# A two-layer diffusion trunk on one core: opening sequence, weight ring and the order of DVE at the norm boundaries changed together

## The chip, the cores and the metric

The kernel runs on one core of a Trainium2 chip. TensorE (PE) multiplies and writes PSUM; VectorE (DVE), ScalarE (ACT) and GpSimd (POOL) do the elementwise work; SyncE (SP) issues nearly all DMAs. The metric is the device time of one execution in microseconds. The kernel before takes 1502.31 us in the median of 3 runs (1501.9 to 1505.26).

## The reference, cut to what matters

384 tokens (128 of context, 256 latent) of width 1024 pass through two layers of three sub-layers each: feed-forward (FFN), mixer, FFN. The mixer of layer 0 is attention beside a convolution, that of layer 1 a Fourier mix beside a gated unit. Everything is float32.

```python
def modulate(x, g, shift, scale):
    return rms_norm(x, g) * (1 + scale) + shift
def swiglu(h, w_in, w_out):
    gate, up = jnp.split(h @ w_in, 2, axis=-1)
    return (jax.nn.silu(gate) * up) @ w_out
def macaron_layer(x, mod, norm_g, ffn_in, ffn_out, mixer):
    m = mod[:, :, None, :]
    x = x + 0.5 * m[:, 2] * swiglu(modulate(x, norm_g[0], m[:, 0], m[:, 1]), ffn_in[0], ffn_out[0])
    mixed, own_kv = mixer(modulate(x, norm_g[1], m[:, 3], m[:, 4]))
    x = x + m[:, 5] * mixed
    x = x + 0.5 * m[:, 8] * swiglu(modulate(x, norm_g[2], m[:, 6], m[:, 7]), ffn_in[1], ffn_out[1])
```

`mod` is `silu(cond) @ w_mod + b_mod`, nine vectors of 1024 for each layer and for each of two conditionings (`c_ctx` for the context, `c` for the latent tokens); FFN_DIM is 2816.

## The kernel before, in words

Activations lie transposed: features on the 128 partitions in KT = 8 tiles, tokens along the free axis. The weights come in 153 units of 128 x 2048 floats (1 MB). To keep float32 precision with the fast float32 form of TensorE, each unit is split: ACT rounds it (`w_hi`, L528), DVE subtracts (`w_lo`, L790). Every product is then three matmuls (function `three`, L1185 to L1187) of 384 columns, so one unit, 16 tiles of 128 x 128, is 48 matmuls. An FFN has 33 units (22 of its first matrix, 11 of its second), mixer 0 has 11, mixer 1 has 10.

Three rings of three buffers hold raw, high and low weights. SP loads unit u when DVE has split unit u-3 (`lo_done`); ACT splits it when it has landed and PE has used unit u-3.

The modulation matrix comes in two ways. The first 18 column tiles come as 9 "pairs" of 1 MB and go through PE (`mod_sums`, L1231, with `mod_columns`, L1241). The other 126 tiles (512 KB each) are multiplied and summed on DVE (`mod_tile`, L812, two instructions for a tile), spread over the FFNs by the tables TILES_BEFORE, TILE_LOOPS and TILES_OUT.

A norm boundary (five of them, numbered 1 to 5; norm 0 is the opening) runs so. The last unit of the sub-layer finishes its eight output tiles one by one (`y_done`); DVE adds each to x (`residual`, L852), ACT squares it (L538), POOL adds six of the squares (L453), PE sums over partitions (L1247), DVE and ACT make 1/rms (L861, L540, L864), DVE writes three diagonal matrices (L865), PE spreads them (L1254), and then DVE (L876), ACT (L546) and DVE (L883) make the operands `a_hi` and `a_lo` tile by tile, on which PE starts the next sub-layer. DVE computes the next shift and scale (`modulation_in`, L835 to L838) behind the residuals, and behind those it splits the second unit of the next sub-layer (`norm_stats(n, unit)`).

The opening brings x in by rows and transposes it on PE (L1350), brings the small vectors in by 13 DMAs from ACT's queue and transposes them (L1360, L1362), computes all 9 pairs, then norm 0, then unit 0. The end transposes x back (L1573), copies it (L773) and stores 3 x 512 KB (L436). The order on each engine is the order in which the code is written; nothing is scheduled by a program.

Of the kernel before, what the change touches and what calls it, by code (L numbers as in the profile page):

```python
# [20 lines left out]
FP32 = mybir.dt.float32  # L21
F32R = mybir.dt.float32r
# [4 lines left out]
P = 128  # L27
# [26 lines left out]
RING = 3  # L54
MRING = 3
UNIT = 2048
# [14 lines left out]
GROUPS_FIRST = 3  # L71
LOOPS = (FT - 1) // RING
FIRST_TILES = MRING * GROUPS_FIRST * PAIR_TILES
MOD_TILES = 2 * MODT - FIRST_TILES
TILES_BEFORE = {0: 3, 2: 0, 3: 0, 5: 2}
TILE_LOOPS = {0: LOOPS, 2: LOOPS, 3: LOOPS, 5: 2}
TILES_OUT = {0: [3, 3] + [2] * 8, 2: [2] + [1] * 9, 3: [3] + [2] * 8 + [0], 5: [0] * 10}
TILE0, _t = {}, 0
for _s in (0, 2, 3, 5):
    TILE0[_s] = _t  # L80
    _t += TILES_BEFORE[_s] + MRING * TILE_LOOPS[_s] + sum(TILES_OUT[_s])
assert _t == MOD_TILES and MRING == RING
# [3 lines left out]
COND_AT = 2 * (MRING - 1)  # L86
# [83 lines left out]
def build(nc, x_prompt, x_sample, cache_k, cache_v, c, c_ctx, b_mod, norm_g,  # L170
          q_norm_g, k_norm_g, conv_w, conv_b, conv_norm_g, conv_norm_b,
          sgu_norm_g, sgu_norm_b, sgu_w, sgu_b, k_ident, k_rope, k_fourier, w_units, w_pairs, w_rows,
          y_prompt, y_sample, new_cache_k, new_cache_v):
    ctx = ExitStack()
    with ctx:
# [117 lines left out]
        out_in, out_t, out_c, out_done = sem("out_in"), sem("out_t"), sem("out_c"), sem("out_done")  # L293
# [38 lines left out]
        def mod_rows(b):  # L332
            return m_raw[:, b, 0:D_MODEL]

        def cond_row(cnd):
            return m_raw[:, cnd, D_MODEL:UNIT]

        def row_products():
            return m_raw[:, 2, D_MODEL:UNIT]
# [3 lines left out]
        def _(sp):  # L343
            def load_unit(u, i=0):

                sp.wait_ge(lo_done, u + 1 + RING * i)
                sp.dma_start(w_raw[:, slot(u), :].unsqueeze(1),
                             w_units[bass.ds(u + i * RING, 1)].rearrange("u p n -> p u n")).then_inc(raw_in[slot(u)], 16)

            def load_pair(group, b, i=0):  # L350

                sp.wait_ge(mod_used, MRING * group + b + 1 + MRING * i)
                sp.dma_start(m_raw[:, b, :].unsqueeze(1),
                             w_pairs[bass.ds(MRING * group + b + i * MRING, 1)].rearrange("u p n -> p u n")
                             ).then_inc(mod_in[b], 16)

            def load_tile(n, i=0):

                if n >= MRING:
                    sp.wait_ge(tile_used, n - MRING + 1 + MRING * i)  # L360
                sp.dma_start(mod_rows(n % MRING).unsqueeze(1),
                             w_rows[bass.ds(n + MRING * i, 1)].rearrange("t p n -> p t n")).then_inc(tile_in[n % MRING], 16)

            def load_ffn(s):
                u0, n = UNIT0[s], TILE0[s]

                if s == 0:
                    for pair in range(MRING, MRING * GROUPS_FIRST):
                        if pair == MRING * GROUPS_FIRST - 2:
                            load_unit(u0)  # L370
                        load_pair(pair // MRING, pair % MRING)
                else:
                    load_unit(u0)
                load_unit(u0 + 1)
                load_unit(u0 + 2)
                if s == 0:
                    sp.wait_ge(mod_used, MRING * (GROUPS_FIRST + 1))
                    for cnd, src in enumerate((c_ctx.unsqueeze(0), c)):
                        sp.dma_start(cond_row(cnd), src.to_broadcast([P, D_MODEL])).then_inc(rows_in, 16)
# [4 lines left out]
                for rounds, with_tiles in ((TILE_LOOPS[s], True), (LOOPS - TILE_LOOPS[s], False)):  # L384
                    if rounds:
                        with sp.Fori(0, rounds) as i:
                            for b in range(RING):
                                load_unit(u0 + 3 + RING * done + b, i)
                                if with_tiles:
                                    load_tile(n + b, i)  # L390
                        done += rounds
                n += MRING * TILE_LOOPS[s]
                for j, tiles in enumerate(TILES_OUT[s]):
                    if j < FFN_OUT_UNITS - 2:
                        load_unit(u0 + FT + 2 + j)
# [3 lines left out]

            sp.dma_start(ident[:], k_ident).then_inc(const_in, 16)  # L400
            sp.dma_start(cond_rows[0:KT, :], c_ctx.rearrange("(r n) -> r n", n=P)).then_inc(cond_in, 16)
            sp.dma_start(cond_rows[KT:2 * KT, :], c[0].rearrange("(r n) -> r n", n=P)).then_inc(cond_in, 16)
            for b in range(MRING):
                load_pair(0, b)
            sp.dma_start(x_nat[:, 0, :], x_prompt[0]).then_inc(x_in, 16)
            sp.dma_start(x_nat[:, 1:TT, :], x_sample[0].rearrange("(a p) n -> p a n", p=P)).then_inc(x_in, 16)
# [26 lines left out]
            for tt in range(TT):  # L433
                sp.wait_ge(out_c, tt + 1)
                dst = y_prompt[0] if tt == 0 else y_sample[0, (tt - 1) * P:tt * P, :]
                sp.dma_start(dst, x_nat[:, tt, :]).then_inc(out_done, 16)  # L436
            sp.wait_ge(out_done, 16 * TT)
# [4 lines left out]
        def _(pool):  # L442
# [12 lines left out]
            add_squares(0)  # L455
# [32 lines left out]
            pool.wait_ge(acc_done, (ADDED - 1) * 5)  # L488
# [1133 lines left out]
```

## Time and profile before

| what | value |
|---|---|
| median of 3 runs | 1502.31 us |
| profiled execution | 1499.5 us, of it span 1497.7 us |
| PE busy | 1407.8 us (94%) |
| DVE busy | 970.0 us (65%) |
| ACT / POOL busy | 557.7 us / 122.5 us |
| chain that ended last | PE 83%, DVE 10%, DMA 2%, ACT 2% |
| granted clock, mean | 0.964 |

A stretch in which PE is busy for its whole length can't be shortened by other engines; where it is not, the row of the timeline names in square brackets the idle time before an instruction and what ended it.

### The profile page before, as it was taken

The page shows a single profiled execution, that of the slowest core. Times are in us where ns is not written, and L with a number is a line of the kernel's source. Part 1 is how long each engine was busy: PE and PEld are TensorE (multiplying, and loading weights), DVE is VectorE, ACT ScalarE, POOL GpSimd, SP SyncE. Part 2 cuts the span into 40 slices and gives each one's busy share as a digit, 9 for nine tenths or more (in the row PEclk, how much of TensorE's full clock was granted, in tenths as well). Part 3 has the DMA queues.
Part 4 walks back from the last instruction along what each step waited for, and adds up shares of the span by engine and source line. Part 5 has one row for each costly group of instructions (what it writes and reads, how often), then busy time and mean ns, then how long its engine had stood idle before and what let it go on. Part 6 is the DMA issues. An engine that isn't in the chain of part 4 may idle for free.

```text
span 1497.7 us, 21193 instructions
## 1 busy us (share of the span) xinstructions
PE 1407.8 (94%) x8134; PEld 1375.4 (92%) x8134; DVE 970.0 (65%) x1394; ACT 557.7 (37%) x731; POOL 122.5 (8%) x110
## 2 busy tenths in 40 slices
PE   5799999989866899999998999999989989999998
PEld 3799999989845799999998999999989989999998
DVE  2777678968998566666757666679763477444332
ACT  2433332237666443333224333332345343333221
POOL 1000000014555100000001000000021010000000
PEclk9899999989878999999998999999989999999999
DMA  8765655752200235555652555547523325433421
GB/s 325 261 231 176 203 177 200 285 182 96 86 32 29 102 133 201 188 191 174 234 181 85 197 193 185 193 149 295 219 99 134 126 85 186 137 122 130 141 84 42
DMA packets 45114, 242.96 MB, mean 162 GB/s; under 512 B 4997, under 2 KB 6889, under 8 KB 24328
## 3 DMA queue, kind: packets, MB, share of 16 engines
q1 hardware_dynamic: 44464, 241.99, 46.7%
q8 instruction: 32, 0.52, 0.1%
q10 hardware_dynamic: 600, 0.30, 0.1%
q14 instruction: 18, 0.15, 0.0%
HBM read 240.57 MB, written 1.70 MB: 162 GB/s over the span
## 4 chain that ended last, share of the span: by engine, by line
PE 83%; DVE 10%; DMA 2%; ACT 2%; issue 1%; POOL 1%; ACTq 0%; SPq 0%; DVEq 0%; POOLq 0%
PE ps L1185 27%; PE ps L1186 27%; PE ps L1187 27%; DVE conv L974 4%; DVE w_lo L790 1%; DMA conv_rows<-in_conv_w 1%; DVE n_full L876 1%; PE ps L1254 1%; DVE m_raw L812 1%; DVE smax L1039 1%; ACT w_hi L528 1%; DVE a_lo L883 0%; POOL n_acc L453 0%; DMA m_raw<-in_w_pairs 0%; PE ps L1554 0%
## 5 line engine op out<-in xcount | busy, mean ns | idle before, releaser
L1185 PE MATMUL ps<-a_hi,w_hi 128*128 128x384 f32 x1744 | 591.7, 339 | 19.1 <-DVE a_lo L883 14.0
L1186 PE MATMUL ps<-a_lo,w_hi 128*128 128x384 f32 x1744 | 588.5, 337 | 0.0
L1187 PE MATMUL ps<-a_hi,w_lo 128*128 128x384 f32 x1744 | 588.1, 337 | 0.0
L790 DVE TENSOR_TENSOR w_lo<-w_raw,w_hi 128x2048 fp32r<-128x2048 f32 x153 | 352.9, 2306 | 162.3 <-ACT w_hi L528 162.0
L528 ACT ACTIVATE w_hi<-w_raw 128x2048 fp32r<-128x2048 f32 x153 | 292.1, 1909 | 264.7 <-PE ps L1187 200.2
L1185 PEld LDWEIGHTS ps<-a_hi,w_hi 128*128 128x128 f32 x1744 | 332.1, 190 | 23.4 <-issue 10.0
L1186 PEld LDWEIGHTS ps<-a_lo,w_hi 128*128 128x128 f32 x1744 | 332.1, 190 | 0.1
L1187 PEld LDWEIGHTS ps<-a_hi,w_lo 128*128 128x128 f32 x1744 | 331.7, 190 | 0.0
L812 DVE SCALAR_TENSOR_TENSOR m_raw<-m_raw 128x1024 f32<-128x1024 f32 x252 | 296.0, 1220 | 1.0 <-ACT m_raw L589 1.0
L1187 PE MATMUL ps<-h_hi,w_lo 128*128 (+1 forms) x704 | 236.6, 336 | 0.0
L1186 PE MATMUL ps<-h_lo,w_hi 128*128 (+1 forms) x704 | 236.6, 336 | 0.0
L1185 PE MATMUL ps<-h_hi,w_hi 128*128 (+1 forms) x704 | 236.6, 336 | 0.0
L557 ACT ACTIVATE glu<-ps 128x384 f32<-128x384 f32 x88 | 43.4, 493 | 376.6 <-PE ps L1187 376.6
L895 DVE TENSOR_TENSOR glu<-glu,ps 128x384 f32<-128x384 f32 x88 | 48.7, 554 | 167.2 <-ACT glu L557 167.2
L1187 PEld LDWEIGHTS ps<-h_hi,w_lo 128*128 128x128 f32 x704 | 132.4, 188 | 0.0
L1185 PEld LDWEIGHTS ps<-h_hi,w_hi 128*128 128x128 f32 x704 | 132.4, 188 | 0.0
L1186 PEld LDWEIGHTS ps<-h_lo,w_hi 128*128 128x128 f32 x704 | 132.4, 188 | 0.0
L898 DVE TENSOR_TENSOR h_lo<-glu,h_hi 128x384 f32 (+1 forms) x88 | 49.2, 559 | 71.6 <-ACT h_hi L559 71.6
L453 POOL TENSOR_TENSOR n_acc<-n_sq 128x384 f32<-128x384 f32 x6 | 6.1, 1014 | 973.4 <-ACT n_sq L538 879.5
L559 ACT ACTIVATE h_hi<-glu 128x384 f32 (+1 forms) x88 | 46.2, 525 | 86.4 <-DVE glu L895 86.4
L473 POOL TENSOR_TENSOR conv<-conv,taps_buf 128x399 f32<-128x399 f32 x60 | 72.9, 1215 | 51.5 <-ACT taps_buf L618 45.6
L974 DVE SCALAR_TENSOR_TENSOR conv<-padded,conv_wt,conv 128x399 f32<-128x399 f32 x60 | 61.1, 1018 | 1.6
(179 smaller groups left out, 666.2 us busy)
## 6 DMA issues: line engine op xcount, KB each, us to landing
w_raw<-in_w_units SPq DMA_DIRECT2D x153, 1024.0 KB, 5.0
m_raw<-in_w_rows SPq DMA_DIRECT2D x126, 512.0 KB, 3.6
m_raw<-in_w_pairs SPq DMA_DIRECT2D x9, 1024.0 KB, 7.7
out<-x_nat SPq DMA_DIRECT2D x3, 512.0 KB, 3.1
x_nat<-in_x_sample SPq DMA_DIRECT2D x1, 1024.0 KB, 12.5
fourier<-in_k_fourier SPq DMA_DIRECT2D x1, 768.0 KB, 4.4
x_nat<-in_x_prompt SPq DMA_DIRECT2D x1, 512.0 KB, 10.7
m_raw<-in_c_ctx SPq DMA_DIRECT2D x1, 512.0 KB, 5.7
```

The costliest lines, as they stand in the source:

```text
L473: nc.gpsimd.tensor_tensor(acc, acc, taps_buf[:, n % TAP_BUFS, :], ALU.add).then_inc(tap_added, 1)
L528: nc.scalar.activation(w_hi[:, slot(u), :], w_raw[:, slot(u), :], ACT.Copy).then_inc(hi_done, 1)
L557: nc.scalar.activation(glu[:, 0, :], ps[:, 2 * b, 0:TOK], ACT.Silu).then_inc(silu_done, 1)
L559: nc.scalar.activation(h_hi[:, bass.ds(t + RING * i, 1), :], glu[:], ACT.Copy).then_inc(h_hi_done, 1)
L790: nc.vector.tensor_tensor(w_lo[:, slot(u), :], w_raw[:, slot(u), :], w_hi[:, slot(u), :].bitcast(FP32), ALU.subtract).then_inc(lo_done, 1)
L812: nc.vector.scalar_tensor_tensor(out, mod_rows(n % MRING), 1.0, cond_row(cnd), ALU.mult, ALU.mult, accum_out=mod_cols[:, bass.ds(FIRST_TIL ...
L895: nc.vector.tensor_tensor(glu[:, 0, :], glu[:, 0, :], ps[:, 2 * b + 1, 0:TOK], ALU.mult).then_inc(prod_done, 1)
L898: nc.vector.tensor_tensor(h_lo[:, bass.ds(t + RING * i, 1), :], glu[:], h_hi[:, bass.ds(t + RING * i, 1), :].bitcast(FP32), ALU.subtract). ...
L974: ins = nc.vector.scalar_tensor_tensor(conv[:, j, :], padded[:, j, k:k + CONV_N], conv_wt[:, j, k:k + 1], conv[:, j, :], ALU.mult, ALU.add)
L1185: mm(out, whi, mhi, start=start, stop=False)
L1186: mm(out, whi, mlo, start=False, stop=False)
L1187: return mm(out, wlo, mhi, start=False, stop=stop)
```

## The change

It does several things in one edit.

1. **Ring.** One ring of four slots in place of three rings of three: `w_lo` lies over `w_raw`, so DVE subtracts in place. A unit is loaded when PE has finished unit u-4 (`unit_done`). The FFN loops turn by four units, and PSUM banks rotate over four steps.
2. **Opening.** Host code hands x, the conditionings and all vectors over already in columns, so the transposes and ACT's 13 DMAs go; the pairs are 8, each with one shift and one scale tile of the same feature tile k; PE works through them one by one between the matmuls of units 0 and 1, which now run together. The squares of norm 0 are all summed on PE.
3. **End.** SP stores x in eight pieces of 192 KB straight behind each residual; no transposes, no copies.
4. **Tiles.** 128 tiles on DVE, 1, 2, 1, 2 in the four steps of a loop; three tiles come in step 1 of FFN 0, not ahead of step 0.
5. **Boundary.** DVE's split of the second unit of the next sub-layer, the gate and `modulation_in` stand ahead of the residuals.

```diff
-RING = 3
+RING = 4
+TRING = 3
+STEP_TILES = [1, 2, 1, 2]
-TILES_BEFORE = {0: 3, 2: 0, 3: 0, 5: 2}
+TILES_BEFORE = {0: TRING, 2: 0, 3: 0, 5: 2}
+TILES_OUT = {0: [2] * 7 + [1, 0, 0], 2: [1, 1] + [0] * 8, 3: [2] * 5 + [0] * 5, 5: [0] * 10}
...
             def load_unit(u, i=0):
-                sp.wait_ge(lo_done, u + 1 + RING * i)
+                sp.wait_ge(unit_done, u + 1 + RING * i)
...
+                    load_pair(0)
+                    load_unit(u0)
+                    load_unit(u0 + 1)
+                    for k in range(1, KT):
+                        load_pair(k)
+                    load_unit(u0 + 2)
...
+            for d in range(KT):
+                sp.wait_ge(x_ready, KT * N_SUB + d + 1)
+                sp.dma_start(y_cols[:, d, :], x[:, d, :]).then_inc(out_done, 16)
...
             norm_stats(0)
             split(0)
-            norm(0)
+            norm(0, 0, 1)
             split(1)
+            norm(0, 1, KT)
+            split(2)
...
+                if s < 5:
+                    split(u0 + FFN_UNITS + 1)
                 modulation_gate(s)
+                if s < 5:
+                    modulation_in(s + 1)
                 for d in range(KT):
...
                     residual(s, d)
-                if s < 5:
-                    modulation_in(s + 1)
...
+            for k in range(KT):
+                if k + 2 < KT:
+                    mod_sums(k + 2)
+                pe.wait_ge(a_ready, k + 1)
+                for m in range(2):
...
+                    for h in range(2):
+                        ins = three(ps[:, 2 * m + h, 0:TOK], tile_of(w_hi, m, h * KT + k), tile_of(w_lo, m, h * KT + k),
+                                    a_hi[:, k, :], a_lo[:, k, :], k == 0, k == KT - 1)
...
+                if k + 2 < KT:
+                    mod_columns(k + 2)
```

DVE's order at the boundary from FFN 0 to mixer 0. Before, the last tiles, the gate, the residuals, shift and scale, then the split:

```order
L790 TENSOR_TENSOR w_lo<-w_raw,w_hi 128x2048
L812 SCALAR_TENSOR_TENSOR m_raw,mod_cols<-m_raw 128x1024 x4
L844 TENSOR_TENSOR m_gate<-mod_cols,vec_a 128x16
L847 TENSOR_SCALAR m_gate<-m_gate 128x16
L852 SCALAR_TENSOR_TENSOR x<-ps,m_gate,x 128x128
...
L835 TENSOR_TENSOR m_shift<-mod_cols,vec_a 128x16
L836 TENSOR_TENSOR m_scale<-mod_cols,vec_a 128x16
L838 SCALAR_TENSOR_TENSOR m_scale<-m_scale,vec_a 128x16
L790 TENSOR_TENSOR w_lo<-w_raw,w_hi 128x2048
L861 TENSOR_SCALAR stat<-ps 128x3
```

In the changed kernel the same place reads (L767 is the split, L789 a tile, L826 a residual, L833 the statistic):

```order
L789 SCALAR_TENSOR_TENSOR m_raw,mod_cols<-m_raw 128x1024 x2
L767 TENSOR_TENSOR w_lo<-w_raw,w_hi 128x2048 x3
L818 TENSOR_TENSOR m_gate<-mod_cols,vec_a 128x16
L821 TENSOR_SCALAR m_gate<-m_gate 128x16
L809 TENSOR_TENSOR m_shift<-mod_cols,vec_a 128x16
L810 TENSOR_TENSOR m_scale<-mod_cols,vec_a 128x16
L812 SCALAR_TENSOR_TENSOR m_scale<-m_scale,vec_a 128x16
L826 SCALAR_TENSOR_TENSOR x<-ps,m_gate,x 128x128
...
L833 TENSOR_SCALAR stat<-ps 128x3
```

The split and the three small instructions went ahead of the sixteen residuals, and no tile is left behind the last two units.

PE's order in the opening. Before:

```order
L1231 MATMUL ps<-m_raw,cond 32x256 x24
L1350 MATMUL ps<-ident,x_nat 128x128 x24
L1241 MATMUL ps<-mod_pick,mod_part 128x6 x2
L1231 MATMUL ps<-m_raw,cond 32x256 x8
L1247 MATMUL ps<-ones,n_sq 128x1 x6
L1247 MATMUL ps<-ones,n_acc 128x1 x3
L1360 MATMUL ps<-ident,rows 128x120
...
L1231 MATMUL ps<-m_raw,cond 32x256 x24
L1241 MATMUL ps<-mod_pick,mod_part 128x6 x2
L1185 MATMUL ps<-a_hi,w_hi 128x384
```

Now (L1224 is a pair's sums, L1234 its columns, L1240 the sum over partitions, L1177 the first matmul of a product):

```order
L1224 MATMUL ps<-m_raw,cond 32x256 x8
L1234 MATMUL ps<-mod_pick,mod_part 128x2 x2
L1240 MATMUL ps<-ones,n_sq 128x1 x24
L1247 MATMUL ps<-n_diag,ones 128x128 x3
L1224 MATMUL ps<-m_raw,cond 32x256 x8
L1234 MATMUL ps<-mod_pick,mod_part 128x2 x2
L1224 MATMUL ps<-m_raw,cond 32x256 x8
L1177 MATMUL ps<-a_hi,w_hi 128x384
...
L1234 MATMUL ps<-mod_pick,mod_part 128x2 x2
L1224 MATMUL ps<-p_raw,cond 32x256 x8
L1177 MATMUL ps<-a_hi,w_hi 128x384
```

The first product now stands behind three pairs, not nine, and five pairs lie between the products.

SP's order in the opening, changed kernel (L350 loads a unit, L354 a pair, L378 the conditioning rows, L360 a tile; the branch opens the loop of FFN 0):

```order
L406 DMA x<-in_x_cols 128x3072
L354 DMA m_raw<-in_w_pairs 128x2048
L350 DMA w_raw<-in_w_units 128x2048 x2
L354 DMA m_raw<-in_w_pairs 128x2048 x2
L354 DMA p_raw<-in_w_pairs 128x2048 x5
L350 DMA w_raw<-in_w_units 128x2048
...
L378 DMA m_raw<-in_c 128x1024
L360 DMA m_raw<-in_w_rows 128x1024 x3
L389 UNCONDITIONAL_BRANCH
```

Before, it read:

```order
L353 DMA m_raw<-in_w_pairs 128x2048 x3
L405 DMA x_nat<-in_x_prompt 128x1024
L406 DMA x_nat<-in_x_sample 128x2x1024
L353 DMA m_raw<-in_w_pairs 128x2048 x4
L347 DMA w_raw<-in_w_units 128x2048
L353 DMA m_raw<-in_w_pairs 128x2048 x2
L347 DMA w_raw<-in_w_units 128x2048 x2
```

x and the first two units moved to the front, and the tile of step 2 is queued ahead of the load of unit 4.

## Rows read from the trace of the kernel before

**Rows 1.** Windows: length, busy of PE, PEld, DVE, ACT, POOL; granted clock; DMA.

```profile
39.00:42.00 3.00, 2.40 (x19) 1.07 (x19) 0.42 (x1) 0.00 (x0) 0.00 (x0) 0.50 0.97 407
160.00:280.00 120.00, 120.00 (x695) 120.00 (x694) 92.71 (x123) 37.72 (x34) 0.00 (x0) 1.00 0.60 203
```

**Rows 2.** Timeline of PE, opening: start, us, engine, line, what, [idle before, releaser].

```profile
7.56 1.93 PE L1231 MATMUL ps<-m_raw,cond 128*32 128x256 f32 x16 [4.03 <-DMA m_raw<-in_w_pairs]
12.71 1.93 PE L1231 MATMUL ps<-m_raw,cond 128*32 128x256 f32 x16 [0.73 <-DMA m_raw<-in_w_pairs]
22.90 1.50 PE L1247 MATMUL ps<-ones,n_sq 128*128 128x1 f32 x12
27.57 1.35 PE L1254 MATMUL ps<-n_diag,ones 128*128 128x128 f32 x6
32.55 0.61 PE L1241 MATMUL ps<-mod_pick,mod_part 128*128 128x6 f32 x4 [0.56 <-DVE mod_part L797]
33.09 1.07 PE L1231 MATMUL ps<-m_raw,cond 128*32 128x256 f32 x16
41.53 1.02 PE L1241 MATMUL ps<-mod_pick,mod_part 128*128 128x6 f32 x4 [0.55 <-DVE mod_part L797]
67.53 0.45 PE L1185 MATMUL ps<-a_hi,w_hi 128*128 128x384 f32 x1 [1.60 <-DVE w_lo L790]
```

**Rows 3.** Timeline of DVE and ACT: one step of FFN 0.

```profile
93.41 0.55 DVE L895 TENSOR_TENSOR glu<-glu,ps 128x384 f32<-128x384 f32 x1 [1.61 <-ACT glu L557]
94.53 1.90 ACT L528 ACTIVATE w_hi<-w_raw 128x2048 fp32r<-128x2048 f32 x1
95.27 1.22 DVE L812 SCALAR_TENSOR_TENSOR m_raw<-m_raw 128x1024 f32<-128x1024 f32 x1
97.56 2.29 DVE L790 TENSOR_TENSOR w_lo<-w_raw,w_hi 128x2048 fp32r<-128x2048 f32 x1
```

**Rows 4.** Timeline, boundary 3 (FFN 2 to FFN 3); last product ends 801.75.

```profile
799.02 4.47 POOL L453 TENSOR_TENSOR n_acc<-n_acc,n_sq 128x384 f32<-128x384 f32 x4
803.83 0.81 PE L1247 MATMUL ps<-ones,n_acc 128*128 128x1 f32 x6
805.97 0.15 DVE L861 TENSOR_SCALAR stat<-ps 128x3 f32<-128x3 f32 x1
811.10 0.66 PE L1185 MATMUL ps<-a_hi,w_hi 128*128 128x384 f32 x1 [2.23 <-DVE a_lo L883]
```

**Rows 5.** Timeline, boundary 1 (FFN 0 to mixer 0); last product ends 325.73.

```profile
322.78 5.29 DVE L852 SCALAR_TENSOR_TENSOR x<-ps,m_gate,x 128x128 f32<-128x128 f32 x16
325.97 6.48 POOL L453 TENSOR_TENSOR n_acc<-n_acc,n_sq 128x384 f32<-128x384 f32 x4
332.50 1.44 PE L1247 MATMUL ps<-ones,n_acc 128*128 128x1 f32 x6 [1.96 <-POOL n_acc L453]
```

**Rows 6.** Timeline of DVE and PE, boundaries 2 (519) and 5 (1207).

```profile
517.48 0.81 PE L1247 MATMUL ps<-ones,n_acc 128*128 128x1 f32 x6
519.48 0.15 DVE L861 TENSOR_SCALAR stat<-ps 128x3 f32<-128x3 f32 x1
1206.52 0.81 PE L1247 MATMUL ps<-ones,n_acc 128*128 128x1 f32 x6
1207.84 0.15 DVE L861 TENSOR_SCALAR stat<-ps 128x3 f32<-128x3 f32 x1
```

**Rows 7.** Timeline, the end; last product ends 1489.07.

```profile
1489.11 0.74 DVE L852 SCALAR_TENSOR_TENSOR x<-ps,m_gate,x 128x128 f32<-128x128 f32 x2 [0.30 <-PE ps L1187]
1491.04 2.86 ACT L773 ACTIVATE x_nat<-ps 128x1024 f32<-128x1024 f32 x3 [24.91 <-PE ps L1573]
```

**Rows 8.** DMA issues, first 75 us and whole span: what, count, KB each, us to landing.

```profile
ident<-in_k_ident SPq DMA_DIRECT2D x1, 64.0 KB, 1.9
...
w_raw<-in_w_units SPq DMA_DIRECT2D x153, 1024.0 KB, 5.0
...
out<-x_nat SPq DMA_DIRECT2D x3, 512.0 KB, 3.1
```

More of the change, by code:

```diff
@@ L432, in _ @@
             load_ffn(5)
[L433 to L437, printed above, removed]
+            for d in range(KT):
+                sp.wait_ge(x_ready, KT * N_SUB + d + 1)
+                sp.dma_start(y_cols[:, d, :], x[:, d, :]).then_inc(out_done, 16)
+            sp.wait_ge(out_done, 16 * KT)
             sp.wait_ge(cache_out, 32)
@@ L540, in norm_stats, with norm @@
                 nc.scalar.activation(stat[:, 4:4 + TT], stat[:, 0:TT], ACT.Sqrt).then_inc(root_done, 1)
-            def norm(n):
-                for d in range(KT):
+            def norm(n, d0=0, d1=KT):
+                for d in range(d0, d1):
                     for cnd, lo, hi in SEGS:
@@ L770, in _ @@
             ffn(5)
-            for tt in range(TT):
-                act.wait_ge(out_t, tt + 1)
-                nc.scalar.activation(x_nat[:, tt, :].rearrange("p (a b) -> p a b", a=2), ps[:, 2 * tt:2 * tt + 2, :],
-                                     ACT.Copy).then_inc(out_c, 1)
         @block.vector
@@ L854, in residual, with norm_stats @@
                 ins.then_inc(x_ready, 1)
-            def norm_stats(n, unit=None):
-                if unit is not None:
-                    split(unit)
+            def norm_stats(n):
                 dve.wait_ge(stat_done, n + 1)
@@ L900, in step @@
                                             ALU.subtract).then_inc(h_ready, 1)
-                    if tile is not None:
+                    for tile in tiles:
                         mod_tile(tile, i)
+                step(0, 0, 0, [])
                 if s == 0:
                     dve.wait_ge(silu_rows, 2)
-                for _ in range(TILES_BEFORE[s]):
-                    mod_tile(n)
-                    n += 1
-                step(0, 0, 0, None)
+                step(1, 1, 0, range(n, n + TILES_BEFORE[s]))
+                n += TILES_BEFORE[s]
                 done = 0
@@ L914, in ffn @@
                             for b in range(RING):
-                                step(1 + RING * done + b, (1 + b) % RING, i, n + b if with_tiles else None)
+                                at = n + sum(STEP_TILES[:b])
+                                step(2 + RING * done + b, (2 + b) % RING, i, range(at, at + STEP_TILES[b] * with_tiles))
                         done += rounds
-                n += MRING * TILE_LOOPS[s]
+                n += sum(STEP_TILES) * TILE_LOOPS[s]
                 for j, tiles in enumerate(TILES_OUT[s]):
@@ L1303, in ffn @@
                 pe.wait_ge(h_ready, 1 + FT * (f + 1))
-                with pe.Fori(0, (FFN_OUT_UNITS - 2) // RING) as i:
+                rounds = (FFN_OUT_UNITS - 2) // RING
+                with pe.Fori(0, rounds) as i:
                     for b in range(RING):
                         out_unit(u0 + FT + 1 + b, 1 + b, i)
+                for t in range(1 + RING * rounds, FFN_OUT_UNITS - 1):
+                    out_unit(u0 + FT + t, t, 0)
                 u = u0 + FFN_UNITS - 1
```

378 lines of the change are left out of this document (173 added, 205 removed).

## The prediction

> **What bounds the kernel now.** I read the page first: PE is busy 94% of the span and holds 83% of the chain, so only stretches in which it waits can give time. The windows then show where it does not wait: from 160 to 280 us PE is busy for all of 120 us, 695 matmuls at 172.7 ns, so a unit of 48 takes 8.3 us [rows 1]. The timeline of PE shows the same for all four FFNs from the fourth unit on, so a deeper ring gains nothing inside an FFN. PE waits in the opening, at five norm boundaries, in the attention and at the end. The attention (DVE and ACT chains) keeps its instructions; I cost it at nothing, since a unit there is loaded earlier than it is split in any case, and DVE, which sets its pace, has the same list.
>
> **The end.** Before, the last residual ends at 1489.85, the last of three copies at 1493.90, and a store of 512 KB takes 3.1 us to land [rows 7, 8]: 1497.0, plus 0.7 to the end of the span. Now the last piece of 192 KB is issued at 1489.9. Its landing lies between the 1.9 us of 64 KB and the 3.1 us of 512 KB [rows 8]; I take 2.3, nearer to the small one. End at 1489.9 + 2.3 + 0.7 = 1492.9: **4.8 us saved** (4.0 to 5.2). The Trainium skill, DMA: Bandwidth & Descriptors, Anatomy of one DMA, gives about 2.0 us fixed plus bytes over 436 GB/s for a DMA from GpSimd's queue, an estimate of 2.45 us here; by it the end would save 4.65 us. No row has a piece of this size.
>
> **The boundaries.** At boundary 3 PE has the sum over partitions done at 803.83 + 0.81 = 804.64, but DVE reads it only at 805.97, because it is still in the split that stands in front [rows 4]. With split and modulation ahead of the residuals DVE reads at once, 0.05 us later: 1.28 saved. Boundary 4 has the same instructions in the same order between two FFN-like stages: 1.28 again. Boundary 2: 519.48 - 518.29 less 0.05 = 1.14. Boundary 5: 1207.84 - 1207.33 less 0.05 = 0.46 [rows 6]. Nothing else is behind DVE there, so what is late next is the unchanged chain of 1/rms, spread and first `a_lo`.
>
> Boundary 1 is different. DVE comes to its residuals only at 322.78, from its tiles, while y's first tile was there 7.3 us before the last product's end, at 318.4 [rows 5]. POOL's four adds then take 6.48 us where boundary 3 has 4.47, and PE's sum is done at 333.94, 8.21 us after its last product; at boundary 3 it is 2.89 us [rows 4, 5]. The new table leaves DVE no tile behind the last three units, so boundary 1 should look like boundary 3: 8.21 - 2.89 = **5.3 saved**. Why POOL is slow matters a little. Its adds lie beside DVE's split, which follows residuals that end at 328.07 [rows 5]; those of boundary 3 lie ahead of the split. The Trainium skill, SBUF — State Buffer, Who interferes with whom, says that a DVE `tensor_tensor` with both inputs in SBUF locks out GpSimd's reads for the whole instruction; the trace agrees, 2.0 us more on four adds. If the adds stayed slow for another reason, the accumulation started on time at 321.9 would end at 329.4 and the sum at 330.2 in place of 328.6, and 3.7 would be saved.
>
> Does the moved split delay the residuals? It needs unit u-4 done, that is two units, 16.6 us, before the boundary's last product ends. Load 5.0 [rows 8], ACT 1.90, DVE 2.29 [rows 3], five small instructions 1.0: ready 10.3 us later with issue time. At an FFN's end the first y comes 9.4 us after that point. DVE starts its residuals 0.9 late, but needs 0.74 for one against 1.04 between two y, and has caught up by the fourth. Behind a mixer the first four residuals wait and the last four do not. Sum of the boundaries: 5.3 + 1.14 + 1.28 + 1.28 + 0.46 = **9.5 us saved** (8 to 10).
>
> **The opening.** Before, PE starts unit 2 at 67.53 [rows 2] and runs on without a gap, so unit 4 starts at 67.53 + 2 x 8.32 = 84.2. Now, in order:
>
> DMA: the first pair landed at 7.56, the third 5.15 later, so 2.58 us for a MB [rows 2]. x (1.5 MB) is first: 8.9. Pair 0 11.4, unit 0 14.0, unit 1 16.6, pair 1 19.2, pair 7 34.7, unit 2 37.3.
>
> PE: pair 0's sums 11.4 to 13.4 (1.93, the slow row), DVE's copy 0.43, columns 1.02 [rows 2]: 15.0. Then the sums of eight tiles of squares. At 2.4 GHz two tiles took 1.50, so eight take 6.0 [rows 2]. At 1.2 GHz one took 1.44 [rows 5], so eight take 11.5; the granted clock of such a stretch is 0.50 in the window at 39 [rows 1]. I take 7.5, near the fast row, since at 22.90 as well PE had just come through other small matmuls. 22.5. Statistic and diagonals 1.2 (805.97 to the spread at boundary 3), spread 1.35 [rows 2]: 25.1. ACT splits unit 0 at 22.9 to 24.8, DVE to 27.1; tile 0 of norm 0 and pair 1's copy to 28.9; columns to 29.95, shift and scale to 30.3. DVE's split of unit 1 ends at 32.6 and the first product starts there.
>
> From there PE is the bound: 96 products' matmuls 16.6, five pairs 5 x 1.07, six columns 6 x 0.61 [rows 2], and 1.7 for the first 3 us at the low clock: 27.3. Units 0 and 1 end at 59.9. The pairs have all landed by 34.7, so the DMAs don't bind. Unit 2 is split by ACT only behind norm 0's last tile, and by DVE behind that: 1.5 us after PE is free, start 61.4.
>
> Then a new wait. Step 1 puts three tiles (3 x 2.29) on DVE. The first is used 10.8 us after unit 2's start, counted in the order of the code: ACT's table load and two SiLU of the conditioning rows end at +1.0, step 0 at +2.6, ACT's split of unit 3 at +4.5, DVE's at +6.8, step 1's product and low part at +8.5, the tile at +10.8 [rows 3]. SP holds the load of unit 4 behind a fourth tile, which waits for that buffer. The load takes 5.5, the splits 4.3 with hand-over: unit 4 starts 20.9 us after unit 2, where PE was free after 16.6. **A stall of 4.3 us.** Unit 4 starts at 82.3 against 84.2: **1.9 saved**. Afterwards DVE needs 15.2 us for two steps (two of 4.15 with one tile, and one tile more [rows 3]) out of 16.6, and works its backlog off; units 5 to 9 come 2 to 4 us ahead of PE's need.
>
> Bounds: without the stall and with fast sums 7.7 saved; with all sums slow (+4.0) and a round trip through DVE of 0.8 us in each of six rounds, 6.9 lost.
>
> **Sum.** 4.8 + 9.5 + 1.9 = 16.2 us. The profiled execution took 1499.5 with 1.8 outside its span; it would take 1483.3. The median of the runs is 2.8 above it, so the time is 1502.3 - 16.2 = 1486.1 us.
>
> **Rivals.**
> (a) The stall at unit 4 does not come, because the load lands sooner or DVE's step 1 is shorter. For it: DMA share is free by then. Against: the tile's wait stands in SP's order. 1502.3 - 20.5 = 1481.8.
> (b) The streamed opening is slow: sums at 1.2 GHz and each round waits for DVE (scale, `a_hi`, `a_lo` in turn). For it: the window at 39 us shows 0.50 for just such pair work [rows 1]. Then the opening loses 6.9 and the time is 1502.3 - 14.3 + 6.9 = 1494.9. The Trainium skill, TensorE: Matmul & The Clock Gate, Part 1, says that the slow clock is the default and activity releases it; by that rule too a thin opening stays slow.
> (c) Slower than before: the FFN loops are no longer free of gaps. A unit is now loaded only once PE has left its slot, and SP holds it behind tiles; DVE has 15.2 of 16.6 us filled in FFN 0, 2 and 3, where it had 2 x 4.15 = 8.3 plus split waits. If contention or register work adds more than 1.4 us to two steps, PE waits. At 1 us too much for each of 30 pairs of steps it costs 30: 1516. Against: DVE's rows are steady to 0.01 us and the unit needed has 8 us of slack in my count.
> (d) The boundary part doesn't do what it says, because the split waits for its load and pushes the residuals: boundaries gain only boundary 1's backlog, 3.7, so 1502.3 - 10.4 = 1491.9.
>
> **How the numbers follow.** Forecast 0.55, (a) 0.15, (b) 0.16, (c) 0.07, (d) 0.07. The forecast's own range is 1482 to 1490. The range of all is 1478 to 1496; it leaves out (c) and the tails of (a) and (b). A change of 0.2%, 3 us, is what a measurement of this kernel can tell from none. Faster: all but (c) and a tenth of (b), 0.91. Same 0.03. Slower 0.06.
>
> **What would show it.** Unit 2 starting near 61 and a PE idle of about 4 us ahead of unit 4, ended by DVE's split and that by a landing; no idle from there to 320. At each boundary, DVE's statistic within 0.1 us of PE's sum, and PE idle plus norm work of about 8.1 us between last and first product in place of 9.35 [rows 4], at boundary 1 too. Residuals of FFN ends 1.04 us apart from the fourth on. The span ending 3 us after the last residual. The forecast is wrong if gaps of PE appear inside FFN 2, 3 or 5, or if the first product starts after 37 us.

## The result, and the profile after

The changed kernel takes 1561.89 us (median of 4 runs, 1556.95 to 1569.81) against 1502.29 us for the kernel before, run beside it: ratio 1.0397, 95% interval 1.0352 to 1.0443. It is slower by 4%, where 1486.1 us, faster than before, was forecast.

I cut the profiled executions at the same places of the program: the start of TensorE's first product and the end of its last one in each sub-layer, and in FFN 0 also the start of unit 4. Times in us; the last column is the kernel of the first experiment, which changes SyncE's order alone.

| stage | before | after | units first |
|---|---|---|---|
| opening, to the start of unit 4 | 84.29 | 85.10 | 80.25 |
| FFN 0 from unit 4 | 241.44 | 283.91 | 241.57 |
| boundary 1 | 13.30 | 7.67 | 7.26 |
| mixer 0 | 176.37 | 177.70 | 180.85 |
| boundary 2 | 9.21 | 8.06 | 7.69 |
| FFN 2 | 277.14 | 289.79 | 276.53 |
| boundary 3 | 9.35 | 8.21 | 8.07 |
| FFN 3 | 277.26 | 305.70 | 277.54 |
| boundary 4 | 9.36 | 8.09 | 7.52 |
| mixer 1 | 106.72 | 106.48 | 106.12 |
| boundary 5 | 8.52 | 8.06 | 8.07 |
| FFN 5 | 276.10 | 276.18 | 277.58 |
| end | 8.64 | 3.05 | 3.06 |
| span | 1497.7 | 1568.0 | 1482.1 |

The boundaries gained 9.6, where 9.5 was forecast, and the end 5.6, where 4.8 was. Three of the four FFNs lost 42.5, 12.7 and 28.4: 83.6 us. They are the three that carry nearly all modulation tiles; FFN 5, with 8 tiles of the 128, lost nothing. Below, the in phase of an FFN is its first 22 units, the out phase its last 11.

The page of the changed kernel, its costliest groups (busy us, mean ns | idle before them, and what ended it). Before, ACT's split waited 264.7 us, 200.2 of them for PE; now it waits for the landing of the unit and for nothing else, while its busy time is as before (292.1 us then):

```profile
L767 DVE TENSOR_TENSOR w_lo<-w_raw,w_hi 128x2048 fp32r<-128x2048 f32 x153 | 352.9, 2309 | 343.9 <-ACT w_hi L512 343.6
L512 ACT ACTIVATE w_hi<-w_raw 128x2048 fp32r<-128x2048 f32 x153 | 292.8, 1914 | 421.3 <-DMA w_raw<-in_w_units 421.3
```

Windows of the changed kernel, columns as in [rows 1]. Where TensorE was busy for all of a window before, it is now busy 65.74 of 79 us at the end of FFN 0 and 67.31 of 75 in FFN 3; in FFN 2's out phase, which has no tiles by then, it is full. The window at 84, around the gap of 4.43 us ahead of unit 4, has the granted clock at 0.50, so this gap costs more than its own length.

```profile
84.00:89.00 5.00, 3.90 (x12) 3.90 (x13) 4.17 (x6) 2.15 (x2) 0.00 (x0) 0.50 0.27 111
290.00:369.00 79.00, 65.74 (x336) 64.18 (x336) 50.51 (x72) 20.20 (x17) 4.07 (x4) 0.91 0.45 173
780.00:850.00 70.00, 70.00 (x406) 70.00 (x405) 22.87 (x24) 19.00 (x15) 2.10 (x3) 1.00 0.37 130
1090.00:1165.00 75.00, 67.31 (x368) 66.37 (x367) 39.47 (x52) 21.49 (x17) 3.04 (x3) 0.95 0.47 174
```

The timeline of PE after, at unit 2, at unit 4 and at four of the 15 gaps of over 0.8 us that lie further inside the FFNs:

```profile
63.74 0.44 PE L1177 MATMUL ps<-a_hi,w_hi 128*128 128x384 f32 x1 [1.23 <-DVE w_lo L767]
85.10 0.69 PE L1177 MATMUL ps<-a_hi,w_hi 128*128 128x384 f32 x1 [4.43 <-DVE w_lo L767]
...
761.44 0.69 PE L1177 MATMUL ps<-h_hi,w_hi 128*128 128x384 f32 x1 [5.69 <-DVE glu L873]
1056.18 0.69 PE L1177 MATMUL ps<-h_hi,w_hi 128*128 128x384 f32 x1 [5.82 <-DVE glu L873]
1085.93 0.68 PE L1177 MATMUL ps<-h_hi,w_hi 128*128 x1 [5.80 <-DVE w_lo L767]
1111.58 0.68 PE L1177 MATMUL ps<-h_hi,w_hi 128*128 x1 [4.12 <-DVE w_lo L767]
```

Each is ended by DVE, by a split or by the last `glu` of an in phase. But DVE was idle before its split, as one unit of FFN 3's out phase shows (timeline of DVE, ACT and SyncE's queue; L789 is a tile's product, L360 issues a tile, L350 a unit):

```profile
1096.43 2.29 DVE L767 TENSOR_TENSOR w_lo<-w_raw,w_hi 128x2048 fp32r<-128x2048 f32 x1 [6.07 <-ACT w_hi L512]
1098.64 1.22 DVE L789 SCALAR_TENSOR_TENSOR m_raw<-m_raw 128x1024 f32<-128x1024 f32 x1
1099.79 1.22 DVE L789 SCALAR_TENSOR_TENSOR m_raw<-m_raw 128x1024 f32<-128x1024 f32 x1
1101.04 0.33 SPq L360 DMA_DIRECT2D m_raw<-in_w_rows  x1
1101.41 0.48 SPq L350 DMA_DIRECT2D w_raw<-in_w_units  x1
1107.18 1.91 ACT L512 ACTIVATE w_hi<-w_raw 128x2048 fp32r<-128x2048 f32 x1 [10.78 <-DMA w_raw<-in_w_units]
1109.13 2.29 DVE L767 TENSOR_TENSOR w_lo<-w_raw,w_hi 128x2048 fp32r<-128x2048 f32 x1 [5.82 <-ACT w_hi L512]
```

Read it as a circle, a chain of waits that closes on itself. Split 2.21, one tile 2.40 to its release, the next tile's issue 0.37, unit issued and landed 5.77, ACT 1.95, and DVE's next split: 12.70 us, against 8.3 that PE needs. The unit stands in SyncE's queue behind a tile, the tile waits for the tile three back, and DVE comes to that one only behind the split of the unit before. No engine is full: DVE idles 5.8 us in each turn. In the in phase, two steps with three tiles turn the same circle in 17.5 us (splits at 1018.40, 1035.97 and 1053.36, the one between each two left out), where PE needs 16.6:

```profile
1018.40 2.29 DVE L767 TENSOR_TENSOR w_lo<-w_raw,w_hi 128x2048 fp32r<-128x2048 f32 x1 [2.35 <-ACT w_hi L512]
...
1035.97 2.29 DVE L767 TENSOR_TENSOR w_lo<-w_raw,w_hi 128x2048 fp32r<-128x2048 f32 x1 [2.50 <-ACT w_hi L512]
...
1053.36 2.29 DVE L767 TENSOR_TENSOR w_lo<-w_raw,w_hi 128x2048 fp32r<-128x2048 f32 x1 [2.32 <-ACT w_hi L512]
```

That eats DVE's lead over PE at 0.9 us per pair of steps, until PE waits for the last `glu` of the in phase: the gaps of 5.69 and 5.82. In the kernel before, the unit needed next was issued one step earlier against the tiles, ahead of them.

### The profile page after: what moved, and what is told of

It reads as the page before. It is cut to its first block, busy times and chain, and to the rows that moved or that the text cites. A ratio compares the mean times of both kernels' runs of the same rounds, so it can differ in the third digit from the quotient of the medians.

```text
span 1568.0 us, 21066 instructions
## 1 busy us (share of the span) xinstructions
PE 1438.7 (92%) x8113; PEld 1398.6 (89%) x8113; DVE 971.6 (62%) x1410; ACT 556.1 (35%) x725; POOL 113.8 (7%) x105
## 4 chain that ended last, share of the span: by engine, by line
PE 46%; DVE 16%; DMA 16%; issue 11%; ACT 8%; SPq 1%; DVEq 1%; POOL 0%; ACTq 0%; POOLq 0%
DMA w_raw<-in_w_units 16%; PE ps L1177 14%; PE ps L1179 14%; PE ps L1178 14%; DVE m_raw L789 6%; ACT w_hi L512 5%; DVE conv L964 4%; DVE w_lo L767 2%; PE ps L1240 1%; DVE glu L873 1%; ACT h_hi L544 1%; SPq L360 1%; DMA m_raw<-in_w_pairs 1%; PE ps L1224 1%; PE ps L1247 1%
## 5 line engine op out<-in xcount | busy, mean ns | idle before, releaser
L1177 PE MATMUL ps<-a_hi,w_hi 128*128 128x384 f32 x1744 | 595.9, 342 | 22.8 <-DVE a_lo L851 11.1
L767 DVE TENSOR_TENSOR w_lo<-w_raw,w_hi 128x2048 fp32r<-128x2048 f32 x153 | 352.9, 2309 | 343.9 <-ACT w_hi L512 343.6
L1177 PEld LDWEIGHTS ps<-a_hi,w_hi 128*128 128x128 f32 x1744 | 333.5, 191 | 35.3 <-DVE w_lo L767 16.1
L789 DVE SCALAR_TENSOR_TENSOR m_raw<-m_raw 128x1024 f32<-128x1024 f32 x256 | 299.2, 1220 | 0.0
L1177 PE MATMUL ps<-h_hi,w_hi 128*128 (+1 forms) x704 | 246.3, 350 | 49.2 <-DVE w_lo L767 32.2
L1178 PE MATMUL ps<-h_lo,w_hi 128*128 (+1 forms) x704 | 243.6, 346 | 0.0
L1179 PE MATMUL ps<-h_hi,w_lo 128*128 (+1 forms) x704 | 243.5, 346 | 0.0
L1177 PEld LDWEIGHTS ps<-h_hi,w_hi 128*128 128x128 f32 x704 | 138.2, 196 | 54.4 <-issue 36.6
L1178 PEld LDWEIGHTS ps<-h_lo,w_hi 128*128 128x128 f32 x704 | 138.3, 196 | 0.0
L1179 PEld LDWEIGHTS ps<-h_hi,w_lo 128*128 128x128 f32 x704 | 137.7, 196 | 0.0
```

The lines of the kernel that those rows point to most:

```text
L767: nc.vector.tensor_tensor(w_lo[:, slot(u), :], w_raw[:, slot(u), :], w_hi[:, slot(u), :].bitcast(FP32), ALU.subtract).then_inc(lo_done, 1)
L789: nc.vector.scalar_tensor_tensor(out, mod_rows(n % TRING), 1.0, cond_row(cnd), ALU.mult, ALU.mult, accum_out=mod_cols[:, bass.ds(FIRST_TIL ...
L1177: mm(out, whi, mhi, start=start, stop=False)
L1178: mm(out, whi, mlo, start=False, stop=False)
L1179: return mm(out, wlo, mhi, start=False, stop=stop)
```

## The experiments

The theory is the circle through SyncE's queue. Rival 1: DVE has too much work. Rival 2: in the ring of four shared slots a load starts only when PE has left the slot, and that is too late. Rival 3 came up later: a unit issued one step later is itself too late, whatever the tiles wait for.

**Units first.**

```diff
+                load_unit(u0 + 3)
                 for _ in range(TILES_BEFORE[s]):
                     load_tile(n)
...
-                                load_unit(u0 + 3 + RING * done + b, i)
+                                load_unit(u0 + 4 + RING * done + b, i)
...
-                    load_unit(u0 + FT + 1 + j)
+                    if j < FFN_OUT_UNITS - 2:
+                        load_unit(u0 + FT + 2 + j)
```

> The changed kernel with SyncE's order alone changed: every unit of an FFN is issued one step earlier against the modulation tiles, so the load of unit t+2 stands ahead of the tiles of step t and no longer behind them. Nothing else moves, the tiles and the work of DVE are the same. Theory (a closed chain through SyncE's queue: a tile's load waits for the tile three back, the unit's load stands behind it, and DVE's use of that tile stands behind the split of the unit): the idle times of PE inside FFN 0, 2 and 3 (42.4, 12.7 and 28.4 us longer than where no tile is) go, and of the 4.4 us ahead of unit 4 about 1 us stays; 1561.9 - 83.5 - 3.3 = 1475 us. Rival 1 (DVE is too full: 15.2 us of work in 16.6, and glu and h_lo come late): DVE's work is the same, so the gaps stay, 1555 to 1562 us. Rival 2 (a load can start only when PE has left the slot, since raw and low part share four slots): that wait is the same, so the gaps stay but for the one ahead of unit 4, about 1558 us.

Measured: 1483.89 us (1480.64 to 1485.47), ratio to before 0.9872 (0.9852 to 0.9891). No gap of PE inside any FFN is left but 1.23 and 0.54 us ahead of units 2 and 4, with DVE's list and the slots unchanged, so rivals 1 and 2 fall as causes of the gaps. Its windows:

```profile
160.00:280.00 120.00, 120.00 (x694) 120.00 (x693) 102.49 (x138) 37.11 (x33) 0.00 (x0) 1.00 0.67 234
290.00:321.00 31.00, 31.00 (x181) 31.00 (x180) 14.80 (x26) 10.32 (x11) 3.38 (x4) 1.00 0.38 132
1010.00:1079.00 69.00, 69.00 (x400) 69.00 (x399) 38.39 (x51) 19.97 (x16) 3.42 (x4) 1.00 0.45 165
```

The span fell from 1568.0 to 1482.1, by 85.9 where I expected 86.8. The time expected (1475) was still 9 us too low, because I took stage losses from the profiled execution, 1569.8 us, off the median of the runs, 1561.9.

**Short tiles.** Only this is edited (the modulation is computed from 64 of its 1024 terms):

```diff
-                        out, mod_rows(n % TRING), 1.0, cond_row(cnd), ALU.mult, ALU.mult,
+                        out[:, 0:64], mod_rows(n % TRING)[:, 0:64], 1.0, cond_row(cnd)[:, 0:64], ALU.mult, ALU.mult,
```

> The changed kernel with each modulation tile's two products on DVE cut from 1024 columns to 64 (the modulation is then computed from 64 of its 1024 terms); loads, waits and order are as in the changed kernel. A tile should take DVE some 0.3 us in place of 2.3. Theory (the chain through SyncE's queue): it still runs load about 6, ACT 1.95, DVE's split 2.2, a short tile 0.3, issue 0.5 = 10.7 to 11 us per unit in the out phase, against PE's 8.3: gaps of PE stay in the out phases of FFN 0 and 3, but shorter, some 2.4 us for each of seven and five units less a lead of up to 8 us, and the in phase has none: 1490 to 1500 us. Rival 1 (DVE too full): DVE has 9 us of 16.6, so no gap is left at all, 1475 to 1480 us. Rival 2 (slots): as before, 1555 us or more.

Measured: 1508.02 us (1505.65 to 1514.22), ratio 1.0042 (1.0028 to 1.0057), 8 us over the theory's range and 28 over rival 1's. Both ranges stood on the base that the first experiment showed to be 9 us too low. The circle turns as worked out, 10.73 and 10.66 us in FFN 0's out phase, with DVE idle for 7.8 of them:

```profile
288.17 2.29 DVE L767 TENSOR_TENSOR w_lo<-w_raw,w_hi 128x2048 fp32r<-128x2048 f32 x1 [7.81 <-ACT w_hi L512]
298.90 2.29 DVE L767 TENSOR_TENSOR w_lo<-w_raw,w_hi 128x2048 fp32r<-128x2048 f32 x1 [7.81 <-ACT w_hi L512]
309.56 2.29 DVE L767 TENSOR_TENSOR w_lo<-w_raw,w_hi 128x2048 fp32r<-128x2048 f32 x1 [7.74 <-ACT w_hi L512]
```

So emptying DVE about halves each turn's excess over 8.3 (from 4.4 to 2.4) and doesn't end it: most of the circle is the load and the two splits. The gaps left inside FFN 0 and 3 are 0.5 to 3.6 us each, 14.6 in sum, and these FFNs take 25 us more than with the units first.

**Late units in the kernel before.** The inverse: in the kernel before, each unit is issued one step later against the tiles.

```diff
                 load_unit(u0 + 1)
-                load_unit(u0 + 2)
...
-                                load_unit(u0 + 3 + RING * done + b, i)
+                                load_unit(u0 + 2 + RING * done + b, i)
...
-                    if j < FFN_OUT_UNITS - 2:
-                        load_unit(u0 + FT + 2 + j)
+                    load_unit(u0 + FT + 1 + j)
```

> The kernel before with SyncE's order alone changed, the other way round: every unit of an FFN from the third on is issued one step later against the tiles, so it stands behind the tiles of the step before, as in the changed kernel. Its three slots, separate raw buffers and one tile per step stay. Theory (the chain through SyncE's queue): the in phase has one tile per step and three tile buffers, so its tile waits three steps back and the loop stays free of gaps; the out phases of FFN 0 (3, 3 and eight times 2 tiles) and FFN 3 (3 and eight times 2) come to 13 to 15 us per unit against 8.3: 25 to 50 us longer in each, 1540 to 1590 us; FFN 2 and 5 within 3 us of before. Rival 1 (DVE too full through 1, 2, 1, 2 tiles) and rival 2 (shared slots): neither is in this kernel, so 1502 to 1506 us.

Measured: 1599.91 us (1598.45 to 1600.92), ratio 1.0648 (1.0628 to 1.0669), 10 us past the upper end. FFN 0 (from its first product) and FFN 3 lost 44.1 and 37.6, inside the 25 to 50 expected of each; the boundaries behind them lost another 11.9 and 3.9, which I had not priced. DVE's splits in FFN 3's out phase stand 12.56 and 12.68 apart, as in the changed kernel, though this one has three rings of three slots:

```profile
1106.33 2.29 DVE L788 TENSOR_TENSOR w_lo<-w_raw,w_hi 128x2048 fp32r<-128x2048 f32 x1 [5.82 <-ACT w_hi L526]
1118.89 2.29 DVE L788 TENSOR_TENSOR w_lo<-w_raw,w_hi 128x2048 fp32r<-128x2048 f32 x1 [5.68 <-ACT w_hi L526]
1131.57 2.29 DVE L788 TENSOR_TENSOR w_lo<-w_raw,w_hi 128x2048 fp32r<-128x2048 f32 x1 [5.81 <-ACT w_hi L526]
```

FFN 2, with one tile per unit (two at one of them), takes 277.1 us (580.94 to 858.04), as before. The late order and several tiles per unit suffice for the loss; the ring of four is not needed for it.

**Six tile buffers.** The changed kernel, SyncE's order as it is:

```diff
-        m_raw = sb("m_raw", [P, MRING, UNIT])
+        m_raw = sb("m_raw", [P, MRING + 2, UNIT])
-TRING = 3
+TRING = 6
-TILES_BEFORE = {0: TRING, 2: 0, 3: 0, 5: 2}
+TILES_BEFORE = {0: 3, 2: 0, 3: 0, 5: 2}
```

with the waits on `tile_used` shifted by six to match. A tile then waits for the tile six back.

> The changed kernel with six buffers for modulation tiles in place of three, and SyncE's order left as it is: each unit's load still stands behind the tiles of the step before. A tile's load now waits until DVE has used the tile six back, three or four steps earlier. Theory (a closed chain, tile used, next tile issued, unit behind it issued, landed, split, tile used): with six buffers the chain closes over three steps instead of one, so the gaps of PE inside FFN 0, 2 and 3 go and the stall ahead of unit 4 shrinks to about 1 us, as with the units issued first: 1480 to 1488 us. Rival 3 (issuing a unit a step later is itself too late, whatever the tiles wait for): gaps stay, 1545 us or more. Rival 2 (slot free only when PE has left it): gaps stay, 1555 us or more.

Measured: 1480.95 us (1480.65 to 1484.04), ratio 0.9862 (0.9847 to 0.9878). The gaps are gone with the units still issued late, so rival 3 falls, rival 2 once more, and the wait of the tile is what closes the circle:

```profile
290.00:320.00 30.00, 30.00 (x175) 30.00 (x174) 13.02 (x23) 10.39 (x11) 3.37 (x4) 1.00 0.37 128
1010.00:1076.00 66.00, 66.00 (x383) 66.00 (x382) 35.30 (x49) 19.54 (x16) 3.69 (x4) 1.00 0.38 128
```

**Units first, residuals first.** DVE's order at all boundaries as before, on top of the first experiment:

```diff
-                if s < 5:
-                    split(u0 + FFN_UNITS + 1)
                 modulation_gate(s)
-                if s < 5:
-                    modulation_in(s + 1)
...
                     residual(s, d)
+                if s < 5:
+                    modulation_in(s + 1)
+                    split(u0 + FFN_UNITS + 1)
```

> The kernel with the units first, and in it DVE's order at all five norm boundaries as in the kernel before: residuals, then the next norm's shift and scale, then the split of the unit. Against the kernel with the units first it prices that part of the change alone. By the prediction's terms: statistic read 1.28 later at boundaries 3 and 4, 1.14 at 2, 0.46 at 5, and 1.28 at boundary 1, whose backlog of tiles is gone in both: 5.4 us slower. Rival (the split ahead of the residuals delays them and gives nothing, or gives more because POOL's adds no longer lie beside the split): within 1 us of it, or 8 to 10 us slower.

Measured: 1485.76 us (1483.82 to 1486.39), ratio 0.9883 (0.9866 to 0.9900): 1.9 us above the units first, which the intervals don't tell from nothing. The traces price the order directly. With the split ahead, DVE reads the statistic 0.04 us after PE's sum at all five boundaries; here it reads it 0.15 after at boundary 1 and 0.51 at the other four. That makes 2.0 us, not 5.4, and agrees with the 1.9 between the medians. (The five boundaries take 8.44, 8.51, 8.53, 8.53 and 8.34, 3.7 more in sum than in the execution of the units first. But with the split ahead the same sum lies anywhere from 38.6 to 40.1 us in the profiled executions of five kernels, so single executions can't price it closer than 2.3 to 3.7.)

So part of what I had priced as DVE's order goes without it. Boundary 3 of the kernel before, and then of this one (ACT's last split ahead of the boundary, its table load, DVE's second small instruction; then PE's sum and the statistic):

```profile
793.53 1.92 ACT L528 ACTIVATE w_hi<-w_raw 128x2048 fp32r<-128x2048 f32 x1 [6.46 <-PE ps L1187]
795.46 1.28 ACT L532 ACT_TABLE_LOAD   x1
802.53 0.99 DVE L836 TENSOR_TENSOR m_scale<-mod_cols,vec_b 128x16 f32<-128x16 f32 x1
```

```profile
783.92 1.92 ACT L514 ACTIVATE w_hi<-w_raw 128x2048 fp32r<-128x2048 f32 x1 [6.35 <-DMA w_raw<-in_w_units]
785.85 1.28 ACT L518 ACT_TABLE_LOAD   x1
796.36 0.16 DVE L812 TENSOR_TENSOR m_scale<-mod_cols,vec_b 128x16 f32<-128x16 f32 x1
797.65 0.81 PE L1241 MATMUL ps<-ones,n_acc 128*128 128x1 f32 x6
798.97 0.15 DVE L835 TENSOR_SCALAR stat<-ps 128x3 f32<-128x3 f32 x1
```

With three slots ACT waits for PE's last unit but one and comes to its first squares 1.5 us after DVE's first residual is done; POOL's adds start 3.9 us before PE's last product ends. With four slots ACT has done its last split earlier and the adds start 4.8 before it. In the kernel before, DVE's m_scale then took 0.99 and ended within 0.03 us of POOL's last add; here, at the end of the adds, it took 0.16. So boundary 3 went from 9.35 to 8.53 without the order, which I put down to the ring (no run changes the ring alone), and to 8.07 with it.

**Opening with POOL's adds.** On top of the units first: GpSimd adds six of norm 0's eight tiles.

```diff
+            add_squares(0)
             add_squares(1)
...
-            for d in range(KT):
-                pe.wait_ge(sq_done, d + 1)
-                ins = token_sums(ps[:, 0, :], n_sq[:, d, :], d, d == KT - 1)
-            ins.then_inc(stat_done, 1)
+            norm_sums(0)
```

> The kernel with the units first, and in it the opening's sums of squares as at the other norms: GpSimd adds six of the eight tiles (five adds of 1.12 us) and TensorE sums three tiles over partitions in place of eight. In the changed kernel eight tiles' sums took 10.4 us on TensorE at the low clock (15.28 to 25.65), where the prediction took 7.5. Theory: the adds lie beside pair 0's products and columns and end near 16.5 to 17 us, the three sums take 3 x 1.3 = 3.9, the statistic is ready near 21, 4.7 us earlier, and all that follows moves with it as far as the pairs have landed: 4 to 5 us off the opening, 1479 to 1480 us. Rival (the opening is held by the landings of the pairs or by the low clock in the rounds that follow, or GpSimd's adds wait for DVE's work of that time): within 1 us of the kernel with the units first, 1483 to 1485 us.

Measured: 1477.09 us (1476.26 to 1479.72), ratio 0.9833 (0.9820 to 0.9847), the fastest of all: 1.7% under the kernel before. The theory's direction and mechanism hold; it expected 4 to 5 us off the kernel with the units first, and 6.8 came. The sums over partitions in the changed kernel, and then in this one:

```profile
15.28 10.38 PE L1240 MATMUL ps<-ones,n_sq 128*128 128x1 f32 x48
```

```profile
14.45 2.70 PE L1243 MATMUL ps<-ones,n_sq 128*128 128x1 f32 x12
17.01 1.42 PE L1243 MATMUL ps<-ones,n_acc 128*128 128x1 f32 x6
```

The sums end at 18.43 in place of 25.83 in the kernel with the units first (7.4 earlier), and unit 4 starts at 74.02 in place of 80.25 (6.2 earlier).

## Why the prediction was wrong, step by step

**The step that failed.** Under rival (c) I wrote "the unit needed has 8 us of slack in my count". I had counted a unit as loaded once PE has left its slot, and named "SP holds it behind tiles" without following that wait. What holds the unit is the tile ahead of it in SyncE's queue, and that tile waits for DVE, which waits for the unit before. A slack against PE means nothing in such a circle: it is 12.7 us long whatever PE does, and from the first turn in which it binds, every unit comes that long after the one before, 4.4 us more than PE needs (the gaps of FFN 3 at 1098.88, 1111.58 and 1124.27 are 12.7 apart). The sign that I had set for being wrong, gaps of PE inside FFN 2, 3 or 5, came in 2 and 3. The two experiments that open it in different places, units first and six tile buffers, bring the same 1481 to 1484 us.

I had the circle in hand. In the opening I wrote that SyncE "holds the load of unit 4 behind a fourth tile" and got a stall of 4.3 us; the trace has 4.43. I treated it as a single event of the opening and did not ask whether the next unit stands behind the next tile. The same reading should have been made for every unit that is issued behind two tiles.

**Rival (c)** named the right place and sign, with a chance of 0.07 and 1 us per pair of steps (1516 us). The in phase loses about that, 0.9. It missed that the out phase, with two tiles for 8.3 us, is much worse: 4.4 us per unit. Its "DVE has 15.2 of 16.6 us filled" was not the cause; the same list runs free of gaps in the first experiment.

**The end.** 4.8 us forecast, 5.6 measured (8.64 to 3.05). The last piece landed sooner than my 2.3: from the end of the last residual to the end of the span it is 2.27 with everything, where I had 3.0, and the eight stores take 1.9 us in the median, as the 64 KB do in [rows 8]. The estimate from the Trainium skill's DMA: Bandwidth & Descriptors, Anatomy of one DMA, 2.45 us, lies further off; the page gives it for GpSimd's queue, these stores are SyncE's, and the measured row decides.

**The boundaries.** 9.5 us forecast; 9.6 measured in the changed kernel (5.63, 1.15, 1.14, 1.27, 0.46) and 11.1 with the units first. Boundary 1's 5.3 from [rows 4, 5] held. The sum is right and its reason half right: boundaries 2 to 5 gained 4.0, and by the experiment DVE's order accounts for 1.9 of it. At boundary 1, 4.9 us came without the order; that they are the tiles no longer ahead of it is argued from the rows, no run changes the table alone. What I had not seen is that the waits of 1.28, 1.28 and 1.14 each contained a small instruction of 0.86 to 0.99 us that takes 0.17 elsewhere, a wait that is gone with four slots even in the old order; the 0.46 of boundary 5 did not contain one. That the sum came out is in part luck.

**The opening.** A gain of 1.9 forecast, a loss of 0.8 measured. The stall was right (4.43 against 4.3). The eight tiles' sums took 10.4 where I took 7.5 "near the fast row"; the slow row, 11.5, was the nearer end. First product at 35.13 against my 32.6, unit 2 at 63.74 against 61.4, unit 4 at 85.10 against 82.3: one error, 2.3 to 2.8 us of it left at each of these places. The Trainium skill, TensorE: Matmul & The Clock Gate, Part 1, has the slow clock as the default until activity releases it; the durations agree with that (below), the column of the granted clock does not show it.

**With the circle opened** the kernel takes 1483.9 us, inside the range of 1478 to 1496 and 2.2 us from the forecast. That nearness is partly luck: opening, boundaries and end gained 20.8 us there, where 16.2 was forecast (the stall at unit 4 was down from 4.4 to 0.5 too), and mixer 0 and FFN 5, put at nothing, took 6.0 back. Still, the one missing wait, 83.6 us, outweighed the whole forecast gain by a factor of five.

**Left open.** Mixer 0, whose instructions I left at nothing, takes 176.37 before, 176.36 with late units, 177.70 after, and 178.3 to 180.9 in the five other kernels. I did not find what sets the 1.3 to 4.5 us. It is also open why the runs of the changed kernel spread over 13 us, where the kernel before spreads over 3.4.

## What to carry to other kernels

Where one queue issues two streams in turn, follow each stream's wait back through its consumer and see whether it returns to the queue. If it does, add up the circle, and compare it with the period of the bounding engine, not with the slack of one transfer. Put the stream that the bounding engine needs ahead of the one that waits on a busy reader, or give the waiting stream enough buffers that it waits on something several turns old. When an event of the opening is worked out and understood, ask at once how often the same code runs. And take a stage's loss off the profiled execution's own time, not off the median.

## What the runs showed of the hardware

- 48 matmuls of one column took 10.38 us at the opening, 216 ns each, where such a group of six takes 0.83 in a boundary, 138 ns each. The weight loads tell why (first a group of 84 to 89 us, just after the stall at unit 4, where the granted clock is 0.50; then the view of the tile n_sq in the opening, durations as minimum, median and maximum; then the window): 333 ns in both, where the mean over the page of the changed kernel is 191. So TensorE ran at its lower level, 1.2 GHz, in the opening, although the granted clock's column says 1.00 for 15 to 26 us. In the opening durations are to be read, not that column.

```profile
L1178 PEld LDWEIGHTS ps<-a_lo,w_hi 128*128 128x128 f32 x4 | 1.3, 333 | 0.0
```

```profile
L1240 PEld LDWEIGHTS ps<-ones,n_sq x48: 333/333/333, 15.2 to 25.2; 128*128 128x128 f32 x48
```

```profile
15.00:26.00 11.00, 10.65 (x50) 10.57 (x50) 0.57 (x3) 0.11 (x2) 0.00 (x0) 1.00 1.01 425
```

- A gap can cost more than its length. FFN 3 lost 28.4 us with 19.3 us of idle (5.82, 5.80, 2.34, 4.12, 1.23). Behind the gaps of 5.82, 5.80 and 4.12 the weight loads took 333 ns for 10, 13 and 18 matmuls, which came 0.32 us apart in place of 0.17: some 6 of the other 9.1 us. Behind the gaps of 2.34 and 1.23 the granted clock stayed at 1.00 and no matmul was slow. The last 3 us I have not broken down.
- A small DVE instruction that began while one of POOL's adds was running ended with that add. In the kernel before this befell one of the three of 16 columns at each of boundaries 1 to 4: L838 took 1.00 and 0.86 us at boundaries 1 and 2, L836 took 0.99 at boundaries 3 and 4, and each ended 0.03 to 0.04 us after an add. At boundary 5, past the last add, none took over 0.18. The other way round, POOL's last add at boundary 1, beside DVE's split of 2.29 us, took 3.06 where the others took 1.0. Boundary 2, POOL's adds and then the instruction, and the same instruction at boundary 5:

```profile
512.72 4.48 POOL L453 TENSOR_TENSOR n_acc<-n_acc,n_sq 128x384 f32<-128x384 f32 x4
516.38 0.86 DVE L838 SCALAR_TENSOR_TENSOR m_scale<-m_scale,vec_a 128x16 f32<-128x16 f32 x1
1205.42 0.18 DVE L838 SCALAR_TENSOR_TENSOR m_scale<-m_scale,vec_a 128x16 f32<-128x16 f32 x1
```

- In the circle, a unit takes 5.8 us from its issue to the start of ACT's split. At boundary 3, ACT's first squares came 1.5 us after the residuals they read in the kernel before, and 0.03 us after them with four slots and the units first: the deeper ring gave time in a place where no transfer was late.
